# Stick-breaking attention with queries on the partitions and backward scans on VectorE

## Chip, cores and metric

The kernel runs on one core of a Trainium2 chip. The metric is the device time of one execution in microseconds (us), the median of several runs. All times below are of that one core.

## What is computed

Two transformer blocks run on one sequence of 512 tokens and width 1024. The second has a stick-breaking attention layer, and only that is touched by the change:

```python
SB_HEADS, SB_HEAD_DIM, Q_BLOCK = 16, 64, 128

def stick_breaking_attention(q, k, v):        # (B, H, S, dh)
    outs = []
    for t0 in range(0, seq, Q_BLOCK):
        t1 = t0 + Q_BLOCK
        z = einsum('bhqd,bhkd->bhqk', q[:, :, t0:t1], k[:, :, :t1]) * scale
        causal = arange(t1)[None, :] < (t0 + arange(Q_BLOCK))[:, None]
        log_stay = where(causal, log_sigmoid(-z), 0.0)
        log_between = cumsum(log_stay, axis=3, reverse=True) - log_stay
        weights = where(causal, exp(log_sigmoid(z) + log_between), 0.0)
        outs.append(einsum('bhqk,bhkd->bhqd', weights, v[:, :, :t1]))
    return concatenate(outs, axis=2)
```

So the logarithm of a weight is the score z less the sum of softplus(z) over this key and all later keys before the query. Queries and keys are normalized by head (rmsnorm with a gain) before that, and the output is multiplied by a square matrix afterwards. Around this layer stand two layers of another block (with softmax attention, half of it a forgetting attention, and a gated MLP), an MLP, a gated recurrence (HGRN2) and another MLP.

## The kernel before

The program is written by engine: each engine has its own list of instructions, and semaphores set the order between them. Activations lie with features on the partitions and the 512 tokens along the free axis. Every projection is a row of *units*: one unit makes 128 output features by 24 matmuls of 128x512 (8 k-tiles, three products each: the high part of the weights with the high and the low part of the activations, and the low part of the weights with the high one), all on L627 in `products`. SP loads a unit's weights, GpSimd rounds them (`round_units`, L578), VectorE makes the low part (`split_low`, L1208). Weights and accumulators have two slots, so that a unit can't start before its slot has been split and the accumulator taken.

The stick-breaking layer has 16 heads in 8 pairs. `sb_pair(pp, par)` is written on TensorE, VectorE and ScalarE. It covers 12 slots (k = 0 to 11), does the attention of pair p (current) and makes Q, K and V of pair p + 1 (following): `share(work, k, ...)` issues 6 of the 72 product matmuls in each slot. The last pair has 30 early matmuls of the output matrix instead, spread over the slots and a tail of 6 more.

Attention of one pair before: keys are on the partitions. Head m = 0 is begun in slot 0, head m = 1 in slot 6.
- TensorE, `scores(m)` (L883): four products of K block b with all queries from that block on, 512, 384, 256 and 128 columns, in three PSUM banks (`Z_PARTS`).
- ScalarE, `softplus_log(m)` (L1859 to L1872): Abs, Exp, Ln for each of three parts.
- VectorE, `stay(m)` (L1402 to L1410): softplus completed, the diagonal block masked (`before01`), and the result split into a rounded high part and a low part, for each of the three parts.
- TensorE, `log_weights(m)` (L894, L899), in slot 5 or 11: it adds a mask and, for each block b and every later block c, minus the sum over later keys, as products with a triangle of minus ones (`neg_incl_r`) or a full tile of minus ones (`neg_ones_r`), for high and low part: 24 matmuls per head.
- ScalarE, `weights(m)` (L1877): Exp into `sb_w`. TensorE, `sb_pv` (L912) and `last_pv` (L945): V times the weights, four products of 128x64 weights and up to 512 columns. VectorE, `sb_output` (L1451, L1453), and ScalarE, `sb_high` (L1907): the output tile of the pair is copied and split.

In the same slots V is transposed on TensorE (slot 2, L932), taken by ScalarE (L1898), and Q and K of the following pair are normalized: `take_raw` (L1417), Square (L1884), a sum by head on TensorE (L938, slots 6 and 10), Ln and Exp (L1887, L1889), `normed` (L1422).

The forgetting attention of the first block, which isn't touched, already has queries on partitions: scores of both heads (L729) and a decay product (L736) per query block, transposes of the weights (L748), and weights times V (L771), in twelve slots beside 72 product matmuls.

Of the kernel before, what the change touches and what calls it, by code (L numbers as in the profile page):

```python
# [21 lines left out]
F32 = mybir.dt.float32  # L22
F32R = mybir.dt.float32r
# [6 lines left out]
P = 128  # L30
S = 512
# [70 lines left out]
Z_AT = [0, 512, 896, 1152]  # L102
Z_N = [512, 384, 256, 128]
Z_W = 1280
Z_BANK = [(0, 0), (1, 0), (2, 0), (2, 256)]

Z_PARTS = [(2, (2, 3), 896, 384), (1, (1,), 512, 384), (0, (0,), 0, 512)]
# [30 lines left out]
SB_STEPS = 40  # L138
SB_ACT_STEPS = 24
# [30 lines left out]
def two_blocks(nc, x, positions, attn_pre_g, w_in, forget_bias, lam_q1, lam_k1, lam_q2, lam_k2, diff_sub_g,  # L170
# [3 lines left out]
    with ExitStack() as ctx:  # L174
# [19 lines left out]
        ident_r = sb("ident_r", [P, P], F32R)  # L194
# [11 lines left out]
        neg_incl_r = sb("neg_incl_r", [P, P], F32R)  # L206
        neg_ones_r = sb("neg_ones_r", [P, P], F32R)
        mask_sb_r = sb("mask_sb_r", [P, P], F32R)
        before01 = sb("before01", [P, P])
# [49 lines left out]
        sb_log = part(4096, Z_W)  # L259
        sb_stay = part(4096 + Z_W, Z_W)  # L260
        sb_w = part(4096 + 2 * Z_W, Z_W)
        sqT = [part(7936 + 512 * i, 512) for i in range(2)]
        skT = [part(8960 + 512 * i, 512) for i in range(2)]
        stay_hi = mid_hi[:, 1].rearrange("p a b -> p (a b)")[:, 0:Z_W]
        stay_lo = mid_lo[:, 1].rearrange("p a b -> p (a b)")[:, 0:Z_W]

# [8 lines left out]
        hdiag = hdiag_t[:]  # L275
        hoff = hoff_t[:]
# [10 lines left out]
        sc = [psum("sc0"), psum("sc1")]  # L287
        tp = [psum("tp0"), psum("tp1")]
# [99 lines left out]
        stay_ready = sem("stay_ready")  # L388
        logw_done = sem("logw_done")
        w_ready = sem("w_ready")  # L390
# [35 lines left out]
        neg_incl_f = scratch[:, 3840:3968]  # L426
        mask_sb_f = scratch[:, 3968:4096]
# [84 lines left out]
        def _(pool):  # L512
# [5 lines left out]
            steps(nc.gpsimd.memset(neg_incl_f, -1.0))  # L518
            steps(nc.gpsimd.memset(mask_sb_f, NEG))
            steps(nc.gpsimd.memset(before01[:], 1.0))  # L520
# [20 lines left out]
            for t in (neg_incl_f, mask_sb_f):  # L541
                nc.gpsimd.affine_select(out=t, in_=t, compare_op=ALU.is_ge, fill=0.0, base=0,
                                        pattern=[[-1, P]], channel_multiplier=1).then_inc(pool_consts, 1)
            nc.gpsimd.affine_select(out=before01[:], in_=before01[:], compare_op=ALU.is_ge, fill=0.0, base=-1,
                                    pattern=[[1, P]], channel_multiplier=-1).then_inc(pool_consts, 1)
# [10 lines left out]
            pool.wait_ge(pool_consts, 7 + len(HALVES))  # L556
# [58 lines left out]
        def _(pe):  # L615
# [246 lines left out]
            def sb_pair(pp, par, current=True, following=True, previous=True, work=()):  # L862
# [10 lines left out]
                def scores(m):  # L873
                    if m == 0:
                        pe.wait_ge(sb_qk_ready, 2 * p + 2)

                    pe.wait_ge(w_ready, 2 * p + m + 1)
                    r = slice(HD * m, HD * m + HD)
                    for bank, blocks, _, _ in Z_PARTS:
                        for b in blocks:  # L880
                            at = Z_BANK[b][1]

                            mm = pe.matmul(z[bank][:, at:at + Z_N[b]], skT[par % 2][r, b * P:b * P + P],  # L883
                                           sqT[par % 2][r, b * P:S], start=(b < 3), stop=True, skip_group_check=True)
                        mm.then_inc(z_done, 1)

                def log_weights(m):

                    for i, (bank, blocks, _, _) in enumerate(Z_PARTS):

                        pe.wait_ge(stay_ready, 6 * p + 3 * m + i + 1)
                        for b in blocks:
                            at = Z_BANK[b][1]
                            pe.matmul(z[bank][:, at:at + P], ident_r[:], mask_sb_r[:], start=False, stop=False,  # L894
                                      skip_group_check=True)
                            for c in range(b, NB):
                                lhs = neg_incl_r if c == b else neg_ones_r
                                for part_ in (stay_hi, stay_lo):
                                    mm = pe.matmul(z[bank][:, at + (c - b) * P:at + Z_N[b]], lhs[:],  # L899
                                                   part_[:, Z_AT[c]:Z_AT[c] + Z_N[c]], start=False,  # L900
                                                   stop=(c == NB - 1), skip_group_check=True)
                        mm.then_inc(logw_done, 1)

                def sb_pv(m, p_):

                    r = slice(HD * m, HD * m + HD)
                    pe.wait_ge(w_ready, 2 * p_ + m + 2)
                    if m == 0:
                        pe.wait_ge(aux_free, aux_n + 1)
                        pe.wait_ge(sb_o_taken, p_ + 1)  # L910
                    for b in range(NB):
                        mm = pe.matmul(po[r, b * P:S], vtok[:, b, r], sb_w[:, Z_AT[b]:Z_AT[b] + Z_N[b]],  # L912
                                       start=(b == 0), stop=(b == NB - 1), skip_group_check=True)
                    mm.then_inc(sb_pv_done, 1)

                for k in range(SLOTS):
                    if current:
                        if k in (0, 6):
                            scores(k // 6)
                        if k == 1 and previous:  # L920
                            last_pv(p - 1)
                        if k == 7:
                            sb_pv(0, p)
                        if k in (5, 11):
                            log_weights(k // 6)
# [14 lines left out]
            def last_pv(p_):  # L940

                pe.wait_ge(w_ready, 2 * p_ + 3)
                r = slice(HD, 2 * HD)
                for b in range(NB):
                    mm = pe.matmul(po[r, b * P:S], vtok[:, b, r], sb_w[:, Z_AT[b]:Z_AT[b] + Z_N[b]],  # L945
                                   start=(b == 0), stop=(b == NB - 1), skip_group_check=True)
                mm.then_inc(sb_pv_done, 1)

            z = [sc[0], sc[1], tp[0]]
            pe.sem_inc(sb_pv_done, 1)  # L950
# [9 lines left out]
            last_pv(PAIRS - 1)  # L960
            for k in range(SLOTS, SLOTS + TAIL):
                share(work, k, SLOTS + TAIL)

# [140 lines left out]
        def _(v):  # L1104
# [48 lines left out]
            TS(neg_ones_r[:], ones[:, 0:P], -1.0, None, ALU.mult)  # L1153
# [8 lines left out]
            v.wait_ge(pool_consts, 7 + len(HALVES))  # L1162
# [229 lines left out]
            def sb_pair(pp, par, current=True, following=True, previous=True):  # L1392
# [4 lines left out]
                def stay(m):  # L1397

                    for i, (bank, blocks, at, n) in enumerate(Z_PARTS):
                        c = slice(at, at + n)  # L1400
                        v.wait_ge(z_log, 6 * p + 3 * m + i + 1)
                        steps(STT(sb_stay[:, c], z[bank][:, 0:n], 0.0, sb_log[:, c], ALU.max, ALU.add))  # L1402
                        steps.wait()
                        for b in blocks:
                            d = sb_stay[:, Z_AT[b]:Z_AT[b] + P]
                            steps(TT(d, d, before01[:], ALU.mult))
                        steps.wait()
                        steps(COPY(stay_hi[:, c], sb_stay[:, c]))
                        steps.wait()
                        TT(stay_lo[:, c], sb_stay[:, c], stay_hi[:, c].bitcast(F32), ALU.subtract).then_inc(stay_ready, 1)  # L1410
# [13 lines left out]
                for k in range(SLOTS):  # L1424
                    if current and k == 0:
                        u = 3 * par + 2
                        take(half + u // 2, u % 2)
                        TT(vraw, acc[u % 2][:], rstd[:], ALU.mult).then_inc(evacuated[u % 2], 1)
                        stay(0)
                    if current and k == 6:  # L1430
                        stay(1)
                    if current and previous and k == 3:
                        sb_output(p - 1)
# [649 lines left out]
```

## Time and profile before

| | us |
|---|---|
| median of 3 runs | 2783.95 |
| lowest, highest | 2780.61, 2784.08 |
| the profiled execution, its own time | 2780.96 |
| span of its profile | 2779.2 |
| TensorE matmul busy | 2668.7 (96%) |
| VectorE busy | 1632.9 (59%) |
| ScalarE busy | 751.9 (27%) |
| GpSimd busy | 461.4 (17%) |

PE is TensorE, PEld its weight load, DVE VectorE, ACT ScalarE, POOL GpSimd. A group of instructions is named by its line, engine, operation and tiles. Matmul records overlap, as they are pipelined, so the length of a piece of work on TensorE is read from the chain (which counts each stretch of time once) and not from the sum of the records. An f32 matmul shows as two instructions. The stick-breaking layer lies between about 1400 and 1700 us.

### The profile page before, as it was taken

Reading aid. Unit: us, or ns where it says so; the run is one execution under the profiler, and the core shown is the slowest. Engines: PE = TensorE matmul, PEld = TensorE weight load, DVE = VectorE, ACT = ScalarE, POOL = GpSimd, SP = SyncE. Lnnn points to the kernel's source line nnn. Section 1 sums busy time; section 2 is a strip of 40 time slices with the busy share of each in tenths; the row PEclk is TensorE's granted clock in tenths of the full one; section 3 lists DMA queues with packets and bytes.
Section 4 is the critical chain, followed back from the end, with each engine's and each line's share of the span. In section 5 each row is a group of like instructions: output and inputs, shape, how many; then the busy total and the mean of one; then the engine's idle time right before and its main releaser. Section 6 shows DMA issues by size and latency. Waiting matters only on the chain.

```text
span 2779.2 us, 38664 instructions
## 1 busy us (share of the span) xinstructions
PE 2668.7 (96%) x12281; PEld 2095.7 (75%) x12281; DVE 1632.9 (59%) x2674; ACT 751.9 (27%) x1450; POOL 461.4 (17%) x463
## 2 busy tenths in 40 slices
PE   6999899999799989999889999999999999999999
PEld 4676688887577668888667777888888887788887
DVE  6765666464675566645555555644547888564452
ACT  2333223120333332211144442100014555310000
POOL 4111121112111111111110001111111111111111
PEclk8999999999899999999999999999999999999999
DMA  3221233333122123333211112333332222233333
GB/s 92 62 61 47 66 101 97 93 98 99 46 61 61 54 68 98 98 97 93 82 38 46 46 46 61 98 98 96 95 96 75 56 60 61 61 98 98 95 95 98
DMA packets 417268, 214.77 MB, mean 77 GB/s; under 512 B 6819, under 2 KB 416014, under 8 KB 417166
## 3 DMA queue, kind: packets, MB, share of 16 engines
q1 hardware_dynamic: 416144, 212.89, 26.6%
q8 instruction: 57, 0.93, 0.1%
q10 hardware_dynamic: 1022, 0.58, 0.1%
q14 instruction: 45, 0.37, 0.0%
HBM read 211.34 MB, written 2.10 MB: 77 GB/s over the span
## 4 chain that ended last, share of the span: by engine, by line
PE 86%; DVE 7%; issue 3%; ACT 2%; DMA 0%; DVEq 0%; POOL 0%; SPq 0%; ACTq 0%; POOLq 0%
PE acc L627 73%; PE sc L729 2%; PE sc L1042 1%; PE sc L899 1%; DVE xT L1335 1%; PE tp L748 1%; PE sc L883 1%; PE po L771 1%; ACT h_hi L1702 1%; PE po L912 1%; DVE w_lo L1208 1%; PE po L945 1%; PE aux L938 1%; PE tp L883 0%; DVE scratch L1145 0%
## 5 line engine op out<-in xcount | busy, mean ns | idle before, releaser
L627 PE MATMUL acc<-h_hi,w_hi 128*128 128x512 f32 x2048 | 840.8, 411 | 52.5 <-DVE h_lo L1137 35.7
L578 POOL TENSOR_SCALAR w_hi<-w_raw 128x1024 fp32r<-128x1024 f32 x398 | 423.7, 1065 | 2296.3 <-PE acc L627 2296.3
L627 PE MATMUL acc<-h_hi,w_lo 128*128 128x512 f32 x2048 | 804.6, 393 | 0.0
L627 PE MATMUL acc<-h_lo,w_hi 128*128 128x512 f32 x2048 | 803.2, 392 | 0.0
L627 PEld LDWEIGHTS acc<-h_hi,w_hi 128*128 128x128 f32 x2048 | 387.4, 189 | 188.2 <-DVE h_lo L1137 52.9
L1208 DVE TENSOR_TENSOR w_lo<-w_raw,w_hi 128x1024 fp32r<-128x1024 f32 x398 | 484.9, 1218 | 67.7 <-POOL w_hi L578 67.3
L627 PEld LDWEIGHTS acc<-h_hi,w_lo 128*128 128x128 f32 x2048 | 387.1, 189 | 84.5
L627 PEld LDWEIGHTS acc<-h_lo,w_hi 128*128 128x128 f32 x2048 | 388.5, 190 | 75.4 <-issue 3.9
L627 PE MATMUL acc<-mid_hi,w_hi 128*128 128x512 f32 x1120 | 439.4, 392 | 5.2 <-DVE mid_lo L1662 3.2
L627 PE MATMUL acc<-mid_lo,w_hi 128*128 128x512 f32 x1120 | 438.3, 391 | 0.0
L627 PE MATMUL acc<-mid_hi,w_lo 128*128 128x512 f32 x1120 | 437.9, 391 | 0.0
L627 PEld LDWEIGHTS acc<-mid_hi,w_hi 128*128 128x128 f32 x1120 | 210.8, 188 | 53.3 <-DVE w_lo L1208 4.5
L627 PEld LDWEIGHTS acc<-mid_lo,w_hi 128*128 128x128 f32 x1120 | 210.9, 188 | 45.3 <-issue 2.7
L627 PEld LDWEIGHTS acc<-mid_hi,w_lo 128*128 128x128 f32 x1120 | 210.6, 188 | 44.4 <-issue 0.7
L1474 DVE TENSOR_TENSOR xT<-xT,acc 128x512 f32 (+1 forms) x80 | 55.0, 687 | 202.5 <-PE acc L627 202.5
L1930 ACT ACTIVATE mid_hi<-scratch 128x512 f32 x64 | 40.5, 633 | 471.9 <-DVE scratch L1513 471.9
L1510 DVE TENSOR_TENSOR scratch<-acc,rstd 128x512 f32<-128x512 f32 x64 | 44.2, 691 | 130.3 <-PE acc L627 121.8
L1275 DVE CUSTOM_DVE_ANT_0 scratch<-sc,mask_row 128x128 f32<-128x128 f32 (+3 forms) x128 | 62.3, 487 | 86.0 <-PE sc L729 46.9
L1770 ACT ACTIVATE scratch<-scratch,stat 128x128 f32<-128x128 f32 (+3 forms) x128 | 72.1, 563 | 133.7 <-DVE stat L1275 133.7
L1828 ACT ACTIVATE mid_hi<-scratch 128x512 f32 x44 | 27.8, 632 | 212.9 <-DVE scratch L1374 212.9
L1368 DVE TENSOR_TENSOR scratch<-acc,rstd 128x512 f32<-128x512 f32 x44 | 30.4, 691 | 84.2 <-PE acc L627 84.2
L1705 ACT ACTIVATE scratch<-yT 128x512 f32 x32 | 20.2, 632 | 208.7 <-DVE yT L1344 137.4
(309 smaller groups left out, 2684.0 us busy)
## 6 DMA issues: line engine op xcount, KB each, us to landing
w_raw<-in_mlp_w_dram SPq DMA_DIRECT2D x128, 512.0 KB, 4.1
w_raw<-in_w_in_dram SPq DMA_DIRECT2D x48, 512.0 KB, 3.9
w_raw<-in_w_gate_dram SPq DMA_DIRECT2D x44, 512.0 KB, 3.8
w_raw<-in_w_up_dram SPq DMA_DIRECT2D x44, 512.0 KB, 3.8
w_raw<-in_w_down_dram SPq DMA_DIRECT2D x32, 512.0 KB, 4.2
w_raw<-in_hg_w_in_dram SPq DMA_DIRECT2D x32, 512.0 KB, 4.1
w_raw<-in_sb_w_qkv_dram SPq DMA_DIRECT2D x24, 512.0 KB, 3.8
w_raw<-in_w_out_dram SPq DMA_DIRECT2D x16, 512.0 KB, 4.1
```

The costliest lines, as they stand in the source:

```text
L578: nc.gpsimd.tensor_scalar(w_hi[:, slot], w_raw[:, slot], 1.0, 1.0, ALU.mult, ALU.mult).then_inc(w_rounded, 1)
L627: mm = pe.matmul(bank[:], w[:, k], r[:, k], start=(k == 0 and i == 0), stop=(k == k_tiles - 1 and i == 2))
L729: mm = pe.matmul(sc[m][:, 0:n], qT[p % 2][r, t * P:t * P + P], kT[p % 2][r, 0:n], start=True, stop=(p < NDIFF))
L748: mm = pe.transpose(tp[ti % 2][:, j * P:j * P + P], src[:, j * P:j * P + P], ident[:])
L1208: TT(w_lo[:, slot], w_raw[:, slot], w_hi[:, slot].bitcast(F32), ALU.subtract).then_inc(w_split, 1)
L1275: v.tensor_tensor_reduce(prob[k % 4][:, 0:n], sc[k % 2][:, 0:n], mask_row[:, S - n:S], 1.0, BIG, ALU.add, ALU.min, stat[:, k % 4:k % 4 + 1 ...
L1368: TT(up, acc[1][:], rstd[:], ALU.mult).then_inc(evacuated[1], 1)
L1474: TT(dst, dst, acc[slot][:], ALU.add).then_inc(evacuated[slot], 1)
L1510: TT(gate, acc[i][:], rstd[:], ALU.mult).then_inc(evacuated[i], 1)
L1770: ACTV(prob[k % 4][:, 0:n], prob[k % 4][:, 0:n], ACT.Exp, bias=stat[:, k % 4:k % 4 + 1], scale=-1.0, accum_out=stat[:, 4 + k % 4:5 + k % 4 ...
L1828: ACTV(mid_hi[:, c % 2, ds(j, 1)], hid, ACT.Copy).then_inc(mid_hi_ready, 1)
L1930: ACTV(mid_hi[:, c % 2, ds(2 * m + i, 1)], hid, ACT.Copy).then_inc(mid_hi_ready, 1)
```

## The change

Queries move onto the partitions. Attention of a pair is now done by query block t = 0 to 3, one every third slot, with both heads in each instruction of VectorE and ScalarE:
- `scores(t)` in slot 3t: for each head one product of 128 queries with the keys up to the block, n = 128(t + 1) columns; the two heads write the two banks of one PSUM pair (`z_pair[t % 2]`).
- `softplus_log(t)` on ScalarE: Abs, Exp, Ln of 2n elements.
- `log_weights(t)` on VectorE in slot 3t + 2: softplus completed; the diagonal block masked by a maximum with a large number; a backward scan for each head (a running sum from the last key to the first; a 0 in `sb_restart` clears the sum at the masked elements); z minus this sum.
- `transposed(p, t)` two steps later (slots 6, 9 and 0, 3 of the next pair): 2(t + 1) transposes of the log weights, into the PSUM pair that held the scores. `sb_exp` on ScalarE makes the weights. `weighted` two slots after the transposes: products with V for each key block and head.
- The sums by triangle on TensorE, the split into high and low parts, and their constants are removed; V has two buffers, since the last two blocks of a pair are done while the next pair runs.
- `sb_output` is parted into `sb_take` and `sb_low`, in slots 6 and 7; `normed(0)` goes from slot 7 to 8. After the last pair the transposes and products of its last two blocks stand in the tail of slots 12 to 17.

```diff
@@ setup
-            for dst, src in ((ident_r, ident[:]), (sel_r, sel_f), (neg_incl_r, neg_incl_f),
-                             (mask_sb_r, mask_sb_f)):
-                nc.gpsimd.tensor_scalar(dst[:], src, 1.0, 1.0, ALU.mult, ALU.mult)
+            nc.gpsimd.tensor_scalar(sel_r[:], sel_f, 1.0, 1.0, ALU.mult, ALU.mult)
-            TS(neg_ones_r[:], ones[:, 0:P], -1.0, None, ALU.mult)
@@ TensorE
-                def scores(m):
-                    if m == 0:
+                def scores(t):
+
+                    step, n = 4 * p + t, (t + 1) * P
+                    if t == 0:
                         pe.wait_ge(sb_qk_ready, 2 * p + 2)
-                    for bank, blocks, _, _ in Z_PARTS:
-                        for b in blocks:
-                            at = Z_BANK[b][1]
+                    if previous or t >= 2:
+
+                        pe.wait_ge(w_ready, step - 1)
+                    for m in range(2):
+                        r = slice(HD * m, HD * m + HD)
+                        pe.matmul(z_pair[t % 2][:, m, 0:n], sqT[par % 2][r, t * P:t * P + P], skT[par % 2][r, 0:n],
+                                  start=True, stop=True).then_inc(z_done, 1)
-                            for c in range(b, NB):
-                                lhs = neg_incl_r if c == b else neg_ones_r
-                                for part_ in (stay_hi, stay_lo):
                 for k in range(SLOTS):
+                    t, behind = k // 3, (k // 3 + 2) % NB
+                    if current and k % 3 == 0 and (previous or t >= 2):
+                        transposed(p if t >= 2 else p - 1, behind)
                     share(work, k, SLOTS if following else SLOTS + TAIL)
+                    if current and k % 3 == 0:
+                        scores(t)
+                    if current and k % 3 == 2 and (previous or t >= 2):
+                        weighted(p if t >= 2 else p - 1, (par if t >= 2 else par - 1) % 2, behind)
+            def transposed(p_, t):
+
+                pe.wait_ge(logw_done, 4 * p_ + t + 1)
+                for m in range(2):
+                    for j in range(t + 1):
+                        mm = pe.transpose(z_pair[t % 2][:, m, j * P:j * P + P], sb_sum[t][:, m, j * P:j * P + P], ident[:])
+                mm.then_inc(wt_done, 1)
+
+            def weighted(p_, par_, t):
+
+                if t == 0:
+                    pe.wait_ge(aux_free, A_SB + 3 + 3 * p_ + 1)
+                    pe.wait_ge(sb_o_taken, p_ + 1)
+                pe.wait_ge(w_ready, 4 * p_ + t + 1)
+                for j in range(t + 1):
+                    for m in range(2):
+                        r = slice(HD * m, HD * m + HD)
+                        mm = pe.matmul(po[r, t * P:t * P + P], sb_vtok[par_][:, j, r], sb_weights[:, m, j * P:j * P + P],
+                                       start=(j == 0), stop=(j == t))
@@ VectorE
+                def log_weights(t):
+
+                    n = (t + 1) * P
+                    v.wait_ge(z_log, 4 * p + t + 1)
+                    soft, total, z = sb_soft[t], sb_sum[t], z_pair[t % 2][:, :, 0:n]
+                    steps(STT(soft, z, 0.0, soft, ALU.max, ALU.add))
+                    steps.wait()
+                    d = soft[:, :, n - P:n]
+                    steps(TT(d, d, sb_mask[:].rearrange("p (m c) -> p m c", m=1).broadcast_to([P, 2, P]), ALU.max))
+                    steps.wait()
+                    for m in range(2):
+                        steps(v.tensor_tensor_scan(total[:, m][:, ::-1], sb_restart[:, S - n:S][:, ::-1], soft[:, m][:, ::-1],
+                                                   0.0, ALU.mult, ALU.add))
+                    steps.wait()
+                    TT(total, z, total, ALU.subtract).then_inc(logw_done, 1)
@@ ScalarE
                 for k in range(SLOTS):
+                    t = k // 3
+                    if current and k % 3 == 0:
+                        if previous or t >= 2:
+                            sb_exp(p if t >= 2 else p - 1, (t + 2) % NB)
+                        if previous and k == 6:
+                            sb_high(p - 1)
+                        softplus_log(t)
+            def sb_exp(p_, t):
+
+                n = (t + 1) * P
+                a.wait_ge(wt_done, 4 * p_ + t + 1)
+                ACTV(sb_weights[:, :, 0:n], z_pair[t % 2][:, :, 0:n], ACT.Exp).then_inc(w_ready, 1)
```

## Rows read from the trace of the kernel before

**Rows 1.** The page, chain that ended last: share of the span by engine.

```profile
PE 86%; DVE 7%; issue 3%; ACT 2%; DMA 0%; DVEq 0%; POOL 0%; SPq 0%; ACTq 0%; POOLq 0%
```

**Rows 2.** The chain in order of time, 1400 to 1710: start us, length us, what.

```profile
1411.58 0.92 PE tp L883 x4
...
1449.36 0.85 PE tp L883 x4
...
1484.79 0.85 PE tp L883 x4
1485.64 1.50 PE sc L883 x4
...
1488.73 2.30 PE po L945 x8
...
1508.96 5.66 PE acc L627 x24
1514.62 1.02 PE aux L938 x2
1515.70 0.46 PE tp L899 x4
...
1518.82 1.43 PE acc L627 x6
...
1662.06 0.85 PE tp L883 x4
...
1691.78 3.23 PE acc L627 x13
```

**Rows 3.** Busy time by stretch: stretch, its us, each engine's busy us, PEclk, DMA.

```profile
860.00:950.00 90.00, 87.44 (x532) 61.60 (x530) 48.73 (x140) 35.19 (x95) 9.30 (x9) 1.00 0.20 53
...
1484.80:1520.30 35.50, 35.50 (x161) 25.07 (x162) 20.26 (x37) 17.05 (x32) 3.14 (x3) 1.00 0.16 45
...
1678.00:1684.00 6.00, 6.00 (x12) 2.52 (x12) 4.29 (x11) 3.22 (x7) 0.00 (x0) 0.50 0.00 0
```

**Rows 4.** The chain again, 875 to 925, a forgetting-attention pair of block one.

```profile
879.37 0.42 PE sc L729 x4
...
891.17 0.37 PE po L771 x4
...
892.13 1.06 PE sc L729 x4
893.19 0.23 PE sc L736 x2
...
901.35 1.03 PE tp L748 x8
...
903.77 1.02 PE po L771 x16
...
906.39 0.42 PE sc L729 x4
```

**Rows 5.** The chain in the first 50 us, one piece.

```profile
34.23 2.32 DVE neg_ones_r L1153
```

**Rows 6.** Groups of instructions by shape, 1395 to 1700: count, busy us, mean ns, idle before.

```profile
L1208 DVE TENSOR_TENSOR w_lo<-w_raw,w_hi 128x1024 fp32r<-128x1024 f32 x25 | 30.4, 1215 | 0.2 <-POOL w_hi L578 0.2
...
L1406 DVE TENSOR_TENSOR scratch<-scratch,before 128x128 f32<-128x128 f32 x64 | 17.2, 289 | 1.7
...
L1402 DVE SCALAR_TENSOR_TENSOR scratch<-sc,scratch 128x512 f32<-128x512 f32 x16 | 10.9, 683 | 0.0
...
L1877 ACT ACTIVATE scratch<-sc 128x512 f32<-128x512 f32 x16 | 9.6, 598 | 12.5 <-PE sc L899 12.5
```

**Rows 7.** The two lines with scans, whole trace: min/median/max ns, shapes.

```profile
L1303 DVE TENSOR_TENSOR_SCAN negc<-ones,yT x2: 1224/1224/1224, 90.0 to 766.9; 128x512 f32<-128x512 f32 x2
...
L1637 DVE TENSOR_TENSOR_SCAN yT<-ones,scratch x32: 395/398/426, 2097.3 to 2344.6; 128x128 f32<-128x128 f32 x32
```

**Rows 8.** VectorE in order of time, one row at 1546 us: start, length, what.

```profile
1546.24 1.54 DVE L1410 TENSOR_TENSOR mid_lo<-scratch,mid_hi 128x512 fp32r<-128x512 f32 x1
```

More of the change, by code:

```diff
@@ L286, in two_blocks @@
         acc = [psum("acc0"), psum("acc1")]
-        sc = [psum("sc0"), psum("sc1")]
-        tp = [psum("tp0"), psum("tp1")]
+        sc_pair, tp_pair = (ctx.enter_context(nc.psum_tensor(name, [P, 2, S], F32)) for name in ("sc", "tp"))
+        sc = [sc_pair[:, i] for i in range(2)]
+        tp = [tp_pair[:, i] for i in range(2)]
+        z_pair = [sc_pair, tp_pair]
         po = psum("po")
@@ L904, in sb_pv @@
[L904 to L914, printed above, removed]
@@ L916, in sb_pair @@
-                for k in range(SLOTS):
[L917 to L925, printed above, removed]
+                    if previous or t >= 2:
+                        pe.wait_ge(w_ready, step - 1)
@@ L938, in sb_pair @@
                             pe.matmul(aux[:], head_ones[:], sb_sq, start=True, stop=True).then_inc(aux_done, 1)
[L940 to L950, printed above, removed]
+            def transposed(p_, t):
[14 more added lines that the diff above has]
+                                       start=(j == 0), stop=(j == t))
+                if t == NB - 1:
+                    mm.then_inc(sb_pv_done, 1)
             sb_pair(0, -1, current=False)
@@ L959, in _ @@
             sb_pair(PAIRS // 2 - 1, 1, following=False, work=work)
-            last_pv(PAIRS - 1)
             for k in range(SLOTS, SLOTS + TAIL):
+                t = 2 + (k - SLOTS) // 3
+                if k % 3 == 0:
+                    transposed(PAIRS - 1, t)
                 share(work, k, SLOTS + TAIL)
+                if k % 3 == 2:
+                    weighted(PAIRS - 1, 1, t)
             def square_matrix(u, rest):
@@ L1395, in sb_pair @@
                 aux_n = A_SB + 3 + 3 * p
[L1397 to L1410, printed above, removed]
+                def log_weights(t):
[12 more added lines that the diff above has]
+                    TT(total, z, total, ALU.subtract).then_inc(logw_done, 1)
                 def take_raw(i):
@@ L1428, in sb_pair @@
                         TT(vraw, acc[u % 2][:], rstd[:], ALU.mult).then_inc(evacuated[u % 2], 1)
[L1429 to L1433, printed above, removed]
                     if following and k == 4:
@@ L1446, in sb_pair, with sb_take, sb_low @@
                         split_low(half + u // 2, u % 2)
-            def sb_output(p):
-                v.wait_ge(sb_pv_done, 2 * p + 3)
+                    if current and previous and k == 6:
+                        sb_take(p - 1)
+                    if current and previous and k == 7:
+                        sb_low(p - 1)
+                    if following and k == 11:
+                        normed(1)
+                    if current and k % 3 == 2:
+                        log_weights(k // 3)
+            def sb_take(p):
+                v.wait_ge(sb_pv_done, p + 1)
                 COPY(sb_orow, po[:]).then_inc(sb_o_taken, 1)
+            def sb_low(p):
                 v.wait_ge(sb_o_hi, p + 1)
                 TT(mid_lo[:, 0, ds(p, 1)], sb_orow, mid_hi[:, 0, ds(p, 1)].bitcast(F32), ALU.subtract).then_inc(sb_o_ready, 1)
-            z = [sc[0], sc[1], tp[0]]
             v.sem_inc(sb_o_taken, 1)
```

112 lines of the change are left out of this document (32 added, 80 removed).

## Prediction

> **What bounds the kernel now.** I read the chain of work that ended last first: TensorE holds 86% of it [rows 1]. The change touches the stick-breaking stage, so next I read that chain there in order of time [rows 2]. Scores of pair 0 start at 1411.58 us, of pair 1 at 1449.36, of pair 2 at 1484.79, of pair 7 at 1662.06, and the first early output unit ends at 1695.01 (1691.78 + 3.23). So pair 0 takes 37.8, each of pairs 1 to 6 takes (1662.06 - 1449.36) / 6 = 35.45, pair 7 with the tail 32.95, together 283.4 us. In a middle pair the chain is TensorE alone, busy 35.50 of 35.50 us, while VectorE is busy 20.26, ScalarE 17.05 [rows 3]. In those pairs a microsecond off TensorE is a microsecond off the time, until another engine comes late. In pair 7 there are only 30 product matmuls to cover the attention chain, and waits decide.
>
> **What leaves TensorE.** Products are 24 matmuls in 5.66 us, 0.236 each [rows 2]; 72 per pair are 17.0. Of the rest, per pair and for both heads:
> - scores: 0.85 + 1.50 = 2.35 a head, 4.7;
> - the masks and triangular sums (L894, L899): from the end of the aux product (1514.62 + 1.02 = 1515.64) to the next products at 1518.82, 3.18 a head, 6.35;
> - weights times V: 2.30 a head, 4.6.
> Sum 15.65. With 17.0 of products that leaves 2.8 for two gain-norm sums (1.02 for one in the row), the V transposes and switching.
>
> **What comes.** The new order of work is, on TensorE, what block one does for a forgetting-attention pair: both heads' scores for one query block on separate row halves, 20 transposes of 128x128, 20 weight-times-V products of 128x64 on separate column halves, 72 products in twelve slots. So I price it by that pair [rows 4]. It runs from 879.37 to 906.39, 27.02 us. The rows show why it is shorter: two 512-column score products take 1.06 us for both heads, where one head's of 512 and 384 took 1.50; 8 products of weights and V (16 instructions) take 1.02; 8 transposes 1.03. From this pair I take off its decay products (L736: four pieces that grow with the query block to 0.23, 0.6 together) and add the two norm sums (1.02 by the row with its switch, 1.9 together). New middle pair without waits: 27.0 - 0.6 + 1.9 = 28.3 us, against 35.45: 7.1 less.
>
> Setup: three roundings and one negated tile go. Of those only the tile counts: it stands on the chain at 34.23 with 2.32 us [rows 5]. The VectorE work behind it slides forward, but some will meet the same GpSimd work, so I book 1 of the 2.3 (bounds 0 and 2.3). A larger memset and a 512-wide select on GpSimd are hidden: it then waits for the first weights.
>
> **VectorE per pair.** A 512-element scalar-tensor-tensor is 0.683, a 128-element tensor-tensor 0.289 [rows 6]: 0.15 + 1.04 ns per element. The scan is 1.224 for 512 and 0.398 for 128 [rows 7]: 0.12 + 2.15 ns per element. For query block t (n = 128(t+1)), two heads at once:
> - softplus sum and final subtraction, 2n elements each: 0.42, 0.68, 0.95, 1.22, together 3.27, twice: 6.5;
> - mask maximum of 256 elements: 0.42, four times: 1.7;
> - two scans of n: 2 x (0.40 + 0.67 + 0.95 + 1.22) = 6.5.
> Sum 14.7, where the old `stay` was 20.26 less about 8.6 of other work (three L1208 of 1.22 [rows 6] and seven tiles of 512 near 0.7), near 12. So VectorE goes from 20.3 to about 23 us per pair while the pair shrinks to 28.3: 81% busy. That the scans read backwards and the mask is broadcast is shown in no row; I bound the scan from 0.5 to 2 times its row and take 1, since direction changes neither element count nor operation.
>
> ScalarE handles the same 10,240 elements of attention per pair in 16 instructions instead of 24 (0.598 for 512 [rows 6]), so it is below its old 17.05. GpSimd's and SP's queues are unchanged in order; weights arrive at the pace that block one's 27 us pair has already had.
>
> **Waits in a middle pair.** The engines run in order, so I lay the three orders beside each other with these durations.
> (a) Scores of block t wait for the exponential of block t-2, since both use the same PSUM pair. Between the transposes and those scores stand six products, 1.42 us; the exponential takes up to 1.03. For t = 3 the exponential stands behind the Square of the next keys on ScalarE, about 0.6 us late: a wait of 0.6.
> (b) The last block's scores come in slot 9. Abs, Exp and Ln of 1024 elements are 3.2 us, so `log_weights(3)` (1.22 + 0.42 + 2.45 + 1.22 = 5.3 us) starts about when the next pair's scores do. Behind it in VectorE's queue are the values of that pair (0.69), for which TensorE's V transposes wait in slot 2, some 5.5 us later: 0 to 0.3 late.
> (c) A row shows a VectorE subtraction that takes 1.54 instead of 0.69 just as GpSimd rounds weights [rows 8]: 0.85 more; I take one such hit per pair. That moves (b) to 0.3 to 0.7.
> The Trainium skill (SBUF — State Buffer, on the shared port pair) says that a VectorE instruction with two SBUF inputs and a GpSimd one that reads SBUF exclude each other fully. The scans have two SBUF inputs, so by that rule each of three roundings (about 1.05 us) could hold VectorE; the trace agrees in kind with the 1.54. By the rule alone the pair would be about 1 us longer than by one such hit, 7 us over the stage.
> Waits together: 1.1 us. Middle pair 29.4.
>
> **Pair 0** has no previous pair's transposes and products, and its old exposed start (37.8 against 35.45) is covered, as the first transposes come only in slot 6: 28.3 less 0.8 + 1.0 of transposes and 0.8 + 1.0 of weighted products is 24.7, and switching and a wait for the first values make it 26.
>
> **Pair 7 and tail** are a chain. Block 1's scores wait for pair 6's last exponential, about 8 us in. From there: scores 0.65, ScalarE 2.0, VectorE 3.1 plus what is queued before it, transposes and exponential 1.5: block 3's scores at about 18.5. Then 1.2 + 3.2 + 5.3, transposes 1.0, exponential 1.03, weighted products 1.1, reach 31. Now nothing hides the output tile's copy, rounding and low part (0.69 + 0.63 + 0.7), then 0.7 for three products: 34.4. TensorE has waits of 2.5 to 3 us in it. In the old pair 7, after a wait, the granted clock was 0.50 in 1678 to 1684 [rows 3], that is 1.2 GHz instead of 2.4, and the f32 products took twice as long. I add 3.6 us for such a stretch (bounds 0 and 8): 38.
> The Trainium skill (TensorE: Matmul & The Clock Gate, Part 4) says that transposes do not count as activity for the clock, which would slow middle pairs as well. The row of block one's forgetting pairs, with the same transposes at a granted clock of 1.00 [rows 3], speaks against it; in pair 7 it would add to the 3.6.
>
> **Sum.** 26 + 6 x 29.4 + 38 = 240.4 against 283.4: 43.0 less, and 1 of setup: 44. The profiled execution took 2780.96 us (span 2779.2), so 2737; the median of the runs is 2783.95, 3 higher. I put the forecast between: 2739 us.
>
> **Rivals.**
> - A, the forecast: TensorE remains the bound with about 1 us of waits. 0.68. Own range: without waits 26 + 6 x 28.3 + 34.4 = 230.2, and 2.3 of setup, is 2725; with 30.5 per pair and 42 at the end, 251, it is 2750.
> - B, VectorE takes over: hits by GpSimd and late orders bring it to 31 to 33 us per pair. 27 + 6 x 32 + 42 = 261, 22 less: 2760. For it: 81% busy, in order, with four waits on ScalarE per pair. Against: in the layout above it idles some 5 us per pair. 0.20.
> - C, better overlap than laid out (waits vanish, pair 7 about 31): 26 + 6 x 28 + 31 = 225 with 2.3 of setup: 2722. 0.06.
> - D, slower: a backward scan costs several times the forward one. VectorE has 23 us without slack; scans are 6.5 of them. At 3.1 times, they add 13.7, a pair is bound by VectorE at 37 plus about 3 of waits, pair 7's chain grows by about 10: 32 + 6 x 40 + 48 = 320, 37 more: 2818. It decides from about 2.3 times on, where the stage equals the old 283. Against it: only the addressing changes. 0.04.
> - E, the change does not do what it says: heads' products don't run side by side, since their semaphore increments or two-bank tiles serialize them. Then scores are 4.7 and weighted products 4.6 again, 3.6 more per pair: 33 per pair, 26 less: 2758 to 2765. For block one, whose form is the same, they do overlap. 0.02.
>
> Range: A, B and C are to be held, up to 2762, down to 2722: 2722 to 2762, about 8 in 10. The measurement tells about 0.2% (5.6 us) from no change. Faster 0.94, within 0.2% 0.02 (D between 2.2 and 2.4 times), slower 0.04.
>
> **What would show it.** In the changed kernel: pairs of 29 to 30 us on the chain; scores of both heads at 1.06 for t = 3, eight transposes in 1.03; VectorE near 23 us per pair; one 512 scan at 1.22; waits on TensorE before the V transposes and before the fourth block's scores only; the last pair 34 to 42 us with TensorE idle half of it. Scans above 1.8 us, or VectorE without idle time in a middle pair, would make the forecast wrong, as would a granted clock below 1 in pairs 1 to 6.

## The result and the profile after

The changed kernel takes 2738.43 us (median of four runs, 2736.87 to 2740.33), the kernel before 2783.84 beside it. The ratio is 0.9842, with a 95% interval of 0.9827 to 0.9857. The profiled execution took 2739.28, its span is 2737.6: 41.6 us less than the 2779.2 before. The forecast was 2739, the range 2722 to 2762.

The page of the changed kernel, busy time and the chain that ended last, by engine (before: [rows 1]):

```profile
PE 2617.0 (96%) x12249; PEld 2058.1 (75%) x12249; DVE 1653.0 (60%) x2625; ACT 745.1 (27%) x1386; POOL 459.5 (17%) x458
...
PE 82%; DVE 8%; ACT 4%; issue 4%; DVEq 0%; DMA 0%; POOL 0%; SPq 0%; ACTq 0%; POOLq 0%
```

TensorE in order of time (start us, length us, what; in brackets how long it waited and for whom), at the first block's scores of pairs 0, 1 and 7:

```profile
1410.26 0.49 PE L874 MATMUL sc<-scratch 64*128 64x128 f32 x4
...
1435.83 0.49 PE L874 MATMUL sc<-scratch 64*128 64x128 f32 x4
...
1612.15 0.49 PE L874 MATMUL sc<-scratch 64*128 64x128 f32 x4 [0.75 <-ACT yT L1870]
```

and the chain at the end of the stage, where the last three products of the first early unit start (0.7 us, so that the stage ends at 1648.5):

```profile
1647.07 0.70 DVE mid_lo L1430
1647.77 0.04 issue
1647.81 44.85 PE acc L618 x189
```

| | before [rows 2] | forecast | after |
|---|---|---|---|
| pair 0 | 37.8 | 26 | 25.6 |
| each of pairs 1 to 6 | 35.45 | 29.4 | 29.39 |
| pair 7 and tail (to 1648.5) | 32.95 | 38 | 36.4 |
| stage | 283.4 | 240.4 | 238.3 |

So the stage gives 45.1 us. It starts 1.3 earlier. The 43.4 us behind it (1695.01 to 1738.39 before) are 0.8 longer. That is 45.6, but between these two traces the span shrank by 41.6 only. The missing 4 are in a place that the change doesn't touch. Busy time by stretch (stretch, its us, busy us of each engine, PEclk, DMA), of the last head of the gated recurrence, from its V transposes to its norm sum, first before and then after:

```profile
2353.50:2378.30 24.80, 19.09 (x110) 14.12 (x109) 18.02 (x46) 13.31 (x27) 0.00 (x0) 1.00 0.07 22
```

```profile
2307.60:2336.30 28.70, 24.52 (x109) 19.56 (x108) 18.25 (x46) 13.31 (x27) 0.00 (x0) 0.76 0.07 19
```

The instructions are the same and VectorE and ScalarE are equally busy. TensorE ran at a mean granted clock of 0.76 instead of 1.00, and the head took 3.9 us more.

The two traces are one execution each, and the execution that was traced before was a short one of its kernel: 2780.96 us, where the median is 2783.84. In 30 further executions of the kernel before, run beside the experiments below, the time goes with the mean granted clock: 2778.05 to 2781.61 us in the eight at 0.985 or more, 2786.16 to 2790.49 in the five at 0.980 or less. The medians differ by 45.4 us, close to the 45.6 above. So the 3.9 us most likely come from which executions were traced, and not from the change.

**Inside a middle pair.** The same view of one pair of the changed kernel (before: [rows 3]):

```profile
1508.90:1538.40 29.50, 28.26 (x159) 19.47 (x158) 22.72 (x31) 16.23 (x24) 3.13 (x3) 1.00 0.19 53
```

TensorE is still the busiest, at a granted clock of 1.00, but 1.24 of the 29.5 us are waits. VectorE has gone from 20.26 to 22.72. TensorE's two waits and its last block of weighted products:

```profile
1516.47 1.13 PE L874 MATMUL tp<-scratch 64*128 64x512 f32 x4 [0.53 <-ACT yT L1870]
...
1529.09 0.66 PE L891 MATMUL aux<-ident,yT 128*128 128x128 f32 x4 [0.71 <-DVE yT L1402]
...
1535.52 1.09 PE L916 MATMUL po<-yT,hdiag_t 128*64 128x128 f32 x16
```

And VectorE just ahead of the second wait:

```profile
1522.15 1.06 DVE L1396 SCALAR_TENSOR_TENSOR scratch<-yT,sb_gain 128x512 f32<-128x512 f32 x1 [1.59 <-ACT yT L1849]
1523.14 1.21 DVE L1375 SCALAR_TENSOR_TENSOR scratch<-tp,scratch 128x1024 f32<-128x1024 f32 x1
1524.38 0.42 DVE L1378 TENSOR_TENSOR scratch<-scratch,sb_mask 128x256 f32<-128x256 f32 x1
1524.84 2.34 DVE L1381 TENSOR_TENSOR_SCAN scratch<-sb_restart,scratch 128x512 f32<-128x512 f32 x2
1527.22 1.22 DVE L1384 TENSOR_TENSOR scratch<-tp,scratch 128x1024 f32<-128x1024 f32 x1
1528.36 0.68 DVE L1402 TENSOR_TENSOR yT<-acc,rstd 128x512 f32<-128x512 f32 x1
```

The fourth block's five instructions fill 1523.14 to 1528.44; the next pair's values (L1402) stand behind them, and the V transposes start when they are done. L1396 takes 1.06 us here and 0.75 elsewhere in the pair. It meets GpSimd's rounding of a unit's weights:

```profile
1521.63 1.04 POOL L571 TENSOR_SCALAR w_hi<-w_raw 128x1024 fp32r<-128x1024 f32 x1 [8.16 <-PE acc L618]
```

The scans' groups by shape (count, busy us, mean ns, idle before), against [rows 7]:

```profile
L1381 DVE TENSOR_TENSOR_SCAN scratch<-sb_restart,scratch 128x512 f32<-128x512 f32 x16 | 18.7, 1211 | 0.3
...
L1381 DVE TENSOR_TENSOR_SCAN scratch<-sb_restart,scratch 128x128 f32<-128x128 f32 x16 | 5.9, 411 | 0.3
```

A backward scan costs what a forward one does: 1.211 against 1.224 us for 512, 0.411 against 0.398 for 128.

### The profile page after: what moved, and what is told of

It reads as the page before. It is cut to its first block, busy times and chain, and to the rows that moved or that the text cites. A ratio compares the mean times of both kernels' runs of the same rounds, so it can differ in the third digit from the quotient of the medians.

```text
span 2737.6 us, 38434 instructions
## 1 busy us (share of the span) xinstructions
PE 2617.0 (96%) x12249; PEld 2058.1 (75%) x12249; DVE 1653.0 (60%) x2625; ACT 745.1 (27%) x1386; POOL 459.5 (17%) x458
## 4 chain that ended last, share of the span: by engine, by line
PE 82%; DVE 8%; ACT 4%; issue 4%; DVEq 0%; DMA 0%; POOL 0%; SPq 0%; ACTq 0%; POOLq 0%
PE acc L618 72%; PE sc L720 2%; PE sc L1016 2%; DVE xT L1308 1%; PE tp L739 1%; PE po L762 1%; ACT h_hi L1679 1%; ACT scratch L1836 1%; DVE scratch L1381 1%; PE tp L874 1%; ACT scratch L1834 1%; DVE w_lo L1181 0%; PE po L1039 0%; DVE scratch L1248 0%; DVE scratch L1375 0%
## 5 line engine op out<-in xcount | busy, mean ns | idle before, releaser
L618 PE MATMUL acc<-h_hi,w_hi 128*128 128x512 f32 x2048 | 846.3, 413 | 49.5 <-DVE h_lo L1111 30.6
```

What stands on the lines that cost most here:

```text
L618: mm = pe.matmul(bank[:], w[:, k], r[:, k], start=(k == 0 and i == 0), stop=(k == k_tiles - 1 and i == 2))
```

## The experiments

All but e9 are edits of the changed kernel. "Pair" is the mean of pairs 2 to 5 (29.46 in the changed kernel; pairs 1 to 6 have 29.39), "last head" the stretch of the recurrence shown above. The diffs show the lines that matter, and the comments in them are added here. The experiments ran in three groups (e1 to e4, e5 to e8, e9 to e12), beside which the kernel before took 2781.90, 2782.44 and 2784.51 us. So whole times of different groups are compared to about 2 us.

**e1: the products of weights and V head by head.**

```diff
-                for j in range(t + 1):
-                    for m in range(2):
+                for m in range(2):
+                    for j in range(t + 1):
```

> The changed kernel with one loop turned: the products of weights and V go head by head instead of alternating between the two column halves; the result is the same. Theory A (TensorE is the bound, and products on separate column halves ran side by side): the sixteen instructions of a fourth block, 1.02 us before, take about 1.7 to 1.8, all blocks of a pair together about 1.7 to 1.9 us more, a middle pair 31.1 to 31.3 us instead of 29.4, the whole 2738 becomes about 2751 to 2753. Rival B (VectorE sets the pace of a middle pair): the 1.8 us fall into TensorE's waits of 0.7 and 0.5 before anything else, and the whole moves by 5 us or less. Rival E (the halves never ran side by side): no change.

Measured: 2738.62 us, pair 29.9, last head 24.9. Blocks three and four of the pair (in the changed kernel 0.88 and 1.09):

```profile
1528.93 1.15 PE L916 MATMUL po<-yT,hdiag_t 128*64 128x128 f32 x12
...
1536.95 1.58 PE L916 MATMUL po<-yT,hdiag_t 128*64 128x128 f32 x16
```

Blocks one and two keep their 0.44 and 0.66. So the order costs TensorE 0.76 us per pair and not 1.8; 0.3 of it disappears in the wait before the V transposes (0.71 to 0.81 becomes 0.44 to 0.54) and 0.46 shows in the pair. A's mechanism is there, its size was wrong by a factor of more than two. The whole didn't move for another reason: in the trace the last head ran at a clock of 1.00 and gave 3.8 us back. The time alone would have been read as "no effect", or as rival B, whose figure (5 us or less) it met.

**e2: both heads' scores on one row half.**

```diff
-                        r = slice(HD * m, HD * m + HD)
+                        r = slice(0, HD)
                         pe.matmul(z_pair[t % 2][:, m, 0:n], ...
```

> The changed kernel, but the second head's scores are computed from the first head's queries and keys, so that both products stand on the same row half (the second head's attention is thereby computed from wrong data). Theory A: a fourth block's scores take 1.9 instead of 1.06 to 1.18, a pair 2.1 us more; a middle pair about 31.5, the whole about 2753 to 2756. Rival B: 5 us or less more. Rival E: no change.

Measured: 2754.84 us, pair 31.34, as A says. On the chain, blocks three and four are

```profile
1546.34 1.50 PE sc L874 x4
...
1554.47 2.00 PE tp L874 x4
```

where the changed kernel has 0.90 and 1.18. Heads on separate row halves are worth 1.9 us per pair and 16 us of the whole (its last head took 30.2 us, 1.5 of these 16). Rivals B and E fall: the scores take 2.0 us more on TensorE, and the pair 1.9 more.

**e3: no scans.**

```diff
-                    for m in range(2):
-                        steps(v.tensor_tensor_scan(total[:, m][:, ::-1], ...))
-                    steps.wait()
-                    TT(total, z, total, ALU.subtract).then_inc(logw_done, 1)
+                    TT(total, z, soft, ALU.subtract).then_inc(logw_done, 1)
```

> The changed kernel without the scans: the log weight is z less this key's own softplus, the sum over later keys is left out. VectorE has 6.5 us per pair less. Theory A: the wait before the V transposes (0.7 per middle pair) goes, the one before the fourth scores (0.5) stays, so a middle pair takes 28.7; pair 7, a chain in which the scans of its blocks stand, takes 30 to 32 instead of 36. The whole about 2728 to 2730. Rival B (VectorE is the bound): middle pairs shorten by 3 us or more only if TensorE has that much waiting; since TensorE has 28.1 us of work in them, B gives at most 2723 and then also a VectorE without idle time in the changed kernel.

Measured: 2726.60 us, pair 28.65, pair 7 to its last weighted product 25.2 us instead of 33.5.

```profile
1519.75:1548.40 28.65, 28.12 (x157) 19.39 (x156) 16.67 (x23) 16.25 (x24) 3.15 (x3) 1.00 0.19 55
```

VectorE has 6 us less and the pair is 0.8 shorter: in middle pairs the scans are hidden but for one wait, as A says. (Of the whole's 12 us less, 1.9 lie ahead of the stage, which starts at 1408.32.) In pair 7, where they stand in a chain, they cost about 8.

**e4: each scan twice.** The loop over `m` runs over (0, 1, 0, 1).

> The changed kernel with each scan issued twice; the result is the same. VectorE has 6.5 us per pair more, 29.2 us of work in all. Theory A, in which VectorE has some 6 us of slack in a pair but stands in the path to the next pair's values: the wait before the V transposes grows by the 2.4 us of the fourth block's scans and by more behind it, a middle pair takes 32.5 to 34 us, pair 7 about 41 to 43, the whole 2765 to 2772. A rival in which the 6 us of slack absorb it: 2742 or less. One in which VectorE was the bound all along: 8 x 6.5 = 52 more, 2790.

Measured: 2775.29 us, pairs 1 to 6 of 34.3, 34.5, 35.7, 32.4, 35.7 and 32.0, pair 7 with tail 45.2. Two of them:

```profile
1476.77:1511.00 34.23, 29.87 (x156) 20.57 (x156) 28.37 (x39) 16.12 (x24) 3.14 (x3) 0.95 0.16 47
1541.30:1573.70 32.40, 28.23 (x157) 19.40 (x156) 27.97 (x38) 16.13 (x24) 3.26 (x3) 1.00 0.17 49
```

and the wait at the V transposes:

```profile
1512.51 0.70 PE L891 MATMUL aux<-ident,yT 128*128 128x128 f32 x4 [2.64 <-DVE yT L1403]
```

Some 5 to 6 us more on VectorE are 2.6 to 6.3 us more per pair: the slack is used up before VectorE is full (28 of 32.4 us busy), since the order of its queue makes TensorE wait 2.1 to 2.7 us before the V transposes and 1.5 to 1.7 before the fourth scores. What A missed is in the clock: two pairs had a granted clock of 0.95, two of 0.90 and two of 1.00, and the four took 2 to 3.5 us more than the two, 11 us together. The whole is 3 to 10 us above A's range.

**e5 and e6: the two waits, one at a time.**

```diff
-                    if current and k == 2:      # V transposes, TensorE
+                    if current and k == 4:
-                    if current and k == 2:      # their copy, ScalarE
+                    if current and k == 5:
```

> The changed kernel with the V transposes moved on TensorE from slot 2 to slot 4 and their copy on ScalarE from slot 2 to slot 5; nothing else. Theory A (of the 29.4 us of a middle pair 0.7 are a wait for VectorE, which has not yet taken the values since the scans of the pair before stand ahead of it): that wait goes, a middle pair takes 28.7 to 28.8, pair 7, in which the same wait is 2.9, takes 1 to 3 us less; stage 6 to 8 us shorter, whole about 2731. Rival F (the wait only moves: VectorE's lateness shows up again at the first block's weighted products or at the first norm sum): pair still 29.2 or more, whole 2737 or more.

Measured: 2739.10 us, pair 29.18, pair 7 to its last weighted product 33.1 instead of 33.5. The wait for values is gone, but the other has grown from 0.53 to 0.84 and 0.88:

```profile
1516.84 1.13 PE L874 MATMUL tp<-scratch 64*128 64x512 f32 x4 [0.88 <-ACT yT L1870]
```

So the wait moved in part: of 0.75 us, 0.35 came back elsewhere. By the figures set beforehand F came true (29.2 or more, 2737 or more) and A didn't (28.7, 2731). The whole shows nothing of what is left: the last head took 29.8.

```diff
                         if previous or t >= 2:
                             sb_exp(p if t >= 2 else p - 1, (t + 2) % NB)
+                        if following and k == 9:
+                            raw_squared(1)      # was in slot 8, ahead of the Exp
```

> The changed kernel with ScalarE's Square of the next keys placed behind the exponential of block 1 instead of ahead of it. Theory A (the other wait, 0.53 us before the fourth block's scores, is for that exponential, which stands behind the Square): the wait goes, a middle pair takes 28.9 instead of 29.4, whole about 2735. Rival F (the Square then comes too late for the norm sum in slot 10, or the softplus of the fourth block late for VectorE): pair unchanged or up to 0.3 longer.

Measured: 2734.56 us, pair 28.85. The wait of 0.53 is gone, as A says.

**e7: both.**

> Both moves at once. Theory A: no wait of TensorE is left in a middle pair, 28.2 us, which is what the forgetting pair of block one gave as the price without waits (28.3); 8 to 9 us over pairs 0 to 6 and 1 to 3 in pair 7, whole about 2727 to 2729. Rival F: the gains don't add, 28.5 or more per pair.

Measured: 2731.71 us, pair 28.25, TensorE without a wait:

```profile
1493.00:1521.20 28.20, 28.11 (x157) 19.35 (x156) 23.21 (x31) 16.23 (x24) 3.18 (x3) 1.00 0.19 57
```

Together the moves give 1.2 us per pair, all of the waits, more than their 0.3 and 0.6 alone: with one wait gone, part of it had shown up in the other. 28.25 is the price without waits, forecast as 28.3 from the forgetting pair of block one. The whole is 3 to 5 us above A's figure, and the last head took 30.3.

**e8, e10 and e11: the recurrence.** e8 adds one unused 512-column product to slot 2 of the last head, e11 one of 128 columns in slots 3 to 9 as well; e10 is the changed kernel unedited.

```diff
                     if current and previous and k == 2:
                         hg_norm(i - 1)
+                        if not following:
+                            pe.matmul(po[:], ones[:, 0:P], ones[:], start=True, stop=True)
+                    if not following and 3 <= k <= 9:
+                        pe.matmul(po[:, 0:P], ones[:, 0:P], ones[:, 0:P], start=True, stop=True)
```

> The changed kernel with one additional f32 product of 512 columns, its result unused, in the last head of the gated recurrence, slot 2, where TensorE waits 1.4 us. Nothing in the stick-breaking stage changes. That last head, untouched by the change, takes 24.8 us from the V transposes to the norm sum in the kernel before and 28.7 in the changed one, with a granted clock of 0.50 for 13 us. Theory G (the clock falls there or not by the activity of TensorE just before, and an execution can go either way): the product keeps the clock at 1.00 and the last head takes about 25, the whole about 2734 to 2735. Rival H (it is the position of the fall in time, which one product does not move): 27 or more in the last head, whole 2737 to 2740.

> The changed kernel once more, unedited, for a second trace. Theory G (the granted clock in the last head of the recurrence can go either way, whatever the stick-breaking stage does): pairs 1 to 6 again 29.4 us, whole 2736 to 2740, and the last head anything from 24.8 to 30.3 us, as in the other traces.

> The changed kernel with products whose result isn't used in the last head of the recurrence: one of 512 columns in slot 2 and one of 128 in each of slots 3 to 9, where TensorE otherwise waits for VectorE in short pieces. One such product in slot 2 alone held the clock at 1.00 for some 10 us longer (27.7 us for the head instead of 28.7). Theory G: with products in every slot the clock stays at 1.00 through the head, 25 to 25.5 us, whole about 2734.5. Rival H (product count doesn't decide it): 27 or more.

Measured: 2738.32, 2740.43 and 2737.09 us, with last heads of 27.7, 29.9 and 25.1. The last head of e10, then of e11:

```profile
2305.80:2335.70 29.90, 26.03 (x111) 21.17 (x109) 18.26 (x46) 13.31 (x27) 0.00 (x0) 0.71 0.07 19
```

```profile
2308.70:2333.80 25.10, 21.07 (x125) 16.43 (x124) 18.11 (x46) 13.31 (x27) 0.00 (x0) 1.00 0.08 23
```

With more TensorE work, the head is 4.8 us shorter. In e8, in windows of 5 us, the clock was 1.00 in the first two and fell in the third; in the changed kernel it fell in the second, so e8 held it some 6 us longer (the 10 us in the expectation of e11 is too much). By the figures set beforehand e8 fell to H (27 or more, 2737 to 2740), e11's head to G, but not its whole. So G isn't settled: it is one trace each, two of eleven traces without added products (table below) also kept 1.00, and e12 below, with the same added products as e11, lost it after 15 us. The times of e11 and e10, taken side by side, are 2736.07 to 2738.76 against 2737.95 to 2742.14.

**e9: the kernel before, with one setup line moved.** `TS(neg_ones_r[:], ones[:, 0:P], -1.0, None, ALU.mult)` stands just ahead of VectorE's stick-breaking stage.

> The kernel before with one line moved: the tile of minus ones is made just ahead of the stick-breaking stage and not in the setup. Theory A (of the 2.3 us that this instruction had on the chain nearly all is a wait for GpSimd, and behind it something else then meets GpSimd): the first low part of weights in the layer loop (48.60 us in the kernel before, 46.93 to 47.24 in nine executions of changed kernels) comes at 47.0 to 47.3, the stick-breaking stage is unchanged at 283 us, the whole 1 to 2 us less, about 2781. Rival (the setup gain belongs to the other removed or changed setup work on GpSimd): 48.4 or later.

Measured: 2782.61 us beside 2784.51, ratio 0.9993 (0.9983 to 1.0002): not told from no change. The chain at the first low part of weights in the layer loop, of the kernel before, the changed one, and e9:

```profile
48.60 1.22 DVE w_lo L1208
```

```profile
47.16 1.22 DVE w_lo L1181
```

```profile
46.79 1.22 DVE w_lo L1207
```

So this one line accounts for the 1.4 us that the change gains in setup. Its last head took 30.6 us at a clock of 0.67, with the old attention ahead of it:

```profile
2354.00:2384.70 30.70, 26.67 (x110) 21.68 (x109) 18.38 (x46) 13.30 (x27) 0.00 (x0) 0.67 0.06 18
```

The last head in all traces without added products:

| kernel | us |
|---|---|
| before, e1 | 24.8, 24.9 |
| e4 | 27.2 |
| changed, e3, e5, e6, e10 | 28.7, 29.7, 29.8, 29.8, 29.9 |
| e2, e7, e9 (old attention) | 30.2, 30.3, 30.6 |

The old attention stands at both ends, and the new one nearly so. So the change isn't needed to lose the clock here; the head varies by up to 5.8 us. The clock was lost in one of two traces with the old attention and in eight of nine with the new one, too few to tell whether the change makes it more frequent. The medians of the whole (45.4 us less, and 44.1 in e10) leave some 1.5 us for that at most.

**e12: moves and added products.** e7 and e11, and six unused products into the free bank `aux` in pair 7: one ahead of the fourth scores, three and two behind the weighted products of the tail.

> Both moves (V transposes in slot 4, Square behind the exponential), the products without use in the recurrence as in the run beside it, and six more of 512 columns in pair 7 and its tail, in waits of 1.7, 3.2 and 2.2 us. Theories A and G: pairs 1 to 6 at 28.2, pair 7 1 us shorter than with the moves alone since its f32 products no longer run at half clock, the recurrence's last head 25 to 25.5 instead of 30.3: 2731.7 - 1 - 5 = about 2726. Rival: the products stand in the way of the chain in pair 7 (each is 0.86 us) and cost as much as the clock gives back there, 2731 or more.

Measured: 2726.67 us (2724.52 to 2728.24), ratio 0.9799 (0.9782 to 0.9815): 58 us less than the kernel before and 14 less than the changed one beside it (e10). Pair 28.25, last head 26.4, more than A and G had set. Pair 7 with tail is 33.6 us, against 35.1 in e7. The fourth block's transposes, first in e7, then here, then in e10, the changed kernel unedited:

```profile
1633.06 1.97 PE L904 MATMUL tp<-ident,scratch 128*128 128x128 f32 x8 [3.19 <-DVE scratch L1384]
```

```profile
1629.65 1.09 PE L911 MATMUL tp<-ident,scratch 128*128 128x128 f32 x8 [0.41 <-DVE scratch L1396]
```

```profile
1640.90 1.09 PE L904 MATMUL tp<-ident,scratch 128*128 128x128 f32 x8 [3.18 <-DVE scratch L1384]
```

The eight transposes take 1.97 us after a wait of 3.19 and 1.09 where unused products fill the wait. But e10 has 1.09 after a wait of 3.18 without any filling. Up to these transposes e12 and e7 take the same time (27.4 us from the start of pair 7). So the 1.5 us between them can't be put down to the filling: they can be an execution that lost the clock against one that didn't.

## Why the prediction was right, and where not

- **The bound and its price.** The price of a pair, taken from another stage that has the same form of work, was 28.3; e7 shows 28.25. In its pieces: scores 3.0 us instead of 4.7, weights times V 2.8 instead of 4.6, 6.35 of masks and triangular sums gone, some 2.9 of transposes new, which is 6.9 of the 7.2 us. TensorE remained the bound of pairs 1 to 6 (A), as e2 shows by adding 2.0 us and getting 1.9.
- **Waits.** Forecast 0.6 and 0.3 to 0.7, measured 0.43 to 0.53 and 0.71 to 0.81. Their places are right. Step (c) has one collision of VectorE with GpSimd per pair, as the trace does, but is wrong in its size: 0.31 us (L1396, 1.06 instead of 0.75), not 0.85. The values are late mainly for the queue: VectorE waits 1.59 us for ScalarE ahead of `normed(1)` (L1396, at 1522.15), and `log_weights(3)` stands behind it and starts at 1523.14, though its own input was ready at 1520.88 (ScalarE's L1838). No run changes this order. From the Trainium skill's rule of the lock (SBUF — State Buffer, on the shared port pair) the prediction worked out up to three holds per pair. The trace agrees with the rule where the two engines meet: L1396 ended at 1523.21, 0.54 us after the rounding, and the instruction of 1.54 us in the kernel before 0.53 after its own. But only one of three roundings met such an instruction. One fell into idle time of VectorE, one on L1391, which reads an accumulator and kept its 0.68, and none on a scan. So the scans' unchanged price (mean 1.211 for 512) is no test of the rule.
- **VectorE.** 23 us forecast, 22.72 measured, with every term near its price. Rival D falls with the 1.211 us of the backward scan, rival B with e2 and e3. Only with the scans doubled (e4) do pairs reach B's 31 to 33 us, and there by waits, with VectorE not yet full.
- **Pair 7.** The chain was forecast to 34.4 without the clock, with 3.6 for the clock: 38. It was 36.4. The term that was too large is the clock. On the chain its f32 work ran at half speed in two places, 0.85, 0.46 and 0.95 us longer than in a middle pair (the eight transposes took 1.72 us, the V transposes ahead of them 1.09, the fourth scores 2.13). That is about 2.3, and the 34.1 left are what was forecast without the clock. In e10, the same kernel, the fourth scores ran at full speed (1.13), and the pair with tail took 35.0, so some 1.4 us of it change between executions. One of the signs was wrong, too: TensorE was busy for 24.8 of the 36.4 us, not half. By the Trainium skill's rule that transposes don't count as activity (TensorE: Matmul & The Clock Gate, Part 4) the prediction worked out a possible slowing of the middle pairs. It didn't come: twenty transposes each, granted clock 1.00. That doesn't refute the rule, since the transposes are some 2.9 us of a pair's 28 us of work. In pair 7, waits and transposes come together, and no run separates them.
- **Setup.** 1 us forecast, 1.4 measured at the layer loop's first weights, and e9 gives as much (1.8) by the tile alone. How much of it reaches the stage can't be told: its first scores start between 1408.1 and 1411.7 in the traces of changed kernels.
- **Side by side.** For scores it is as the rows said. For weights times V the order of heads is worth 0.76 us per pair (e1), where I had put the whole step from 4.6 to 2.8 down to the halves. What makes the other 1 us isn't shown by any run.
- **The sum.** By the traces the stage gave 2.1 us more than forecast, mostly in pair 7 (1.6), and setup 0.3 more, while the stretch behind the stage and the last head took 4.7 back, which nothing in the sum foresaw. The forecast was put 2 us above its own sum, since the traced execution before was 3 below the median. Those 3 us and the 3.9 of the last head are probably of one kind, since the executions of one kernel differ in time as they do in granted clock. By the medians the kernel lost 45.4 us where the sum had 44. So the mechanism and the sum are right within 1.4 us, and it is luck that 2739 met 2738.43 within 0.6.

## What to carry to other kernels

Price a rewritten stage by another stage of the same kernel that already has its form: here it gave the time without waits to 0.1 us. Then lay the engines' in-order queues beside each other for the waits, and try their cures together, since a wait that is cured alone can come back in part at the next one. And when a whole time moves by less than expected, compare the untouched stages as well, and a second execution of the same kernel: a stretch whose granted clock falls in some executions and holds in others took or gave up to 5.8 us here, and made an experiment look as if it did nothing.

## What was not expected of the hardware

- A stretch of unchanged instructions (the last head) ran at a granted clock of 1.00 in some traces and fell to 0.50 in others: 24.8 to 30.6 us. TensorE was busy for 19.1 of the 24.8 us. With seven products of 128 columns and one of 512 without use it took 25.1 (e11) and 26.4 (e12). In two executions of one kernel the same scores in pair 7 took 2.08 us (clock 0.50) and 1.13 (e10).
- A VectorE instruction that met a GpSimd rounding ended 0.53 to 0.54 us after it: 1.54 us instead of 0.69 where both started together (before), 1.06 instead of 0.75 where the rounding had started 0.52 us earlier (after).
- f32 products with 64-column weights, issued head by head, take 94 ns per instruction in a block of 16 (1.51 us on the chain, two instructions per product) and 64 ns when they alternate between column halves (1.02). In blocks of 12 the records are 1.15 and 0.88 us, and in blocks of 4 and 8 there is no difference.
